# A macaron layer with attention and HGRN on one core: other orders in the SwiGLU and mix queues

## The reference

```python
x = x + 0.5 * swiglu_ffn(rms_norm(x, g1), w_gate1, w_up1, w_down1)    # D_FF = 2816
proj = rms_norm(x, gm) @ w_in                                          # 7 x 512 columns
aq, ak, av, hq, hf, hi, hg = split(proj)
A = chunked_band_attention(rms_norm(aq), rms_norm(ak), av, rel_bias)   # 8 heads x 64, 9-chunk key band
B = rms_norm(hgrn2(silu(hq), 1 - f, hi, log f)) * silu(hg)             # 4 heads x 128
x = x + concat(A, B) @ w_out
x = x + 0.5 * swiglu_ffn(rms_norm(x, g2), w_gate2, w_up2, w_down2)
```

## Time and profile before

| | us |
|---|---|
| runs of the kernel before | 1912.31, 1910.54, 1912.07 (median 1912.07) |
| the profiled execution | 1910.18 |
| its span in the trace | 1908.6 |
| busy in the span: PE / DVE / ACT / POOL | 1872.8 / 1130.3 / 675.0 / 419.2 |
| start, until the first product | 0 to 16.3 |
| FFN1: gate and up, then down | 16.3 to 457, then to 683 |
| mix | 683 to 1045 |
| attention | 1046 to 1167 |
| W_OUT, then FFN2 | 1168.7 to about 1270, then to the end |

### The profile page before, as it was taken

How to read it: one execution, slowest core, us unless ns; L and a number is a source line. 1 busy time by engine, 2 the same in 40 slices (tenths; PEclk the granted TensorE clock), 3 DMA queues, 4 the chain that set the end, 5 groups by cost and what they waited for, 6 DMA issues and landing times.

```text
span 1908.6 us, 24404 instructions
## 1 busy us (share of the span) xinstructions
PE 1872.8 (98%) x9160; PEld 1545.2 (81%) x9160; DVE 1130.3 (59%) x1583; ACT 675.0 (35%) x1027; POOL 419.2 (22%) x327
## 2 busy tenths in 40 slices
PE   9899999999999999999999999999999999999999
PEld 7688888888888888888887667887888888888887
DVE  6866666665556631157567774367666666655564
ACT  7332323233433534211223663263323232334332
POOL 2322342232103110002222310003224322421030
PEclk9999999999999999999999999999999999999999
DMA  5454545445866433433433510134545354468663
GB/s 169 149 175 151 169 140 177 149 149 210 338 195 196 130 122 117 137 115 132 137 121 99 175 59 1 47 108 149 177 149 177 133 183 143 155 224 315 221 192 138
DMA packets 221483, 297.04 MB, mean 156 GB/s; under 512 B 15392, under 2 KB 117928, under 8 KB 221376
## 3 DMA queue, kind: packets, MB, share of 16 engines
q1 hardware_dynamic: 206752, 262.19, 40.3%
q0 software_dynamic: 6272, 18.14, 2.9%
q10 hardware_dynamic: 8352, 15.27, 2.1%
HBM read 206.65 MB, written 92.56 MB: 157 GB/s over the span
## 4 chain that ended last, share of the span: by engine, by line
PE 91%; DVE 4%; issue 2%; ACT 1%; DMA 1%; POOL 0%; SPq 0%; DVEq 0%; ACTq 0%
PE ps L702 28%; PE ps L703 28%; PE ps L704 28%; PE ps L904 1%; PE ps L1001 1%; PE ps L736 1%; PE ps L988 1%; PE ps L1021 1%; DVE hK L1934 0%; PE ps L924 0%; DMA xs<-x 0%; PE ps L895 0%; DVE PT L2030 0%; DVE S L2019 0%; PE ps L927 0%
## 5 line engine op out<-in xcount | busy, mean ns | idle before, releaser
L702 PE MATMUL ps<-hThi,whi 128*128 128x512 f32 x896 | 350.8, 391 | 11.6 <-DVE hid L1685 9.8
L703 PE MATMUL ps<-hTlo,whi 128*128 128x512 f32 x896 | 349.4, 390 | 0.0
L704 PE MATMUL ps<-hThi,wlo 128*128 128x512 f32 x896 | 349.2, 390 | 0.0
L702 PE MATMUL ps<-whi 128*128 128x512 f32 x616 | 240.0, 390 | 0.0
L704 PE MATMUL ps<-whi,wlo 128*128 128x512 f32 x616 | 239.7, 389 | 0.0
L703 PE MATMUL ps<-wlo,whi 128*128 128x512 f32 x616 | 239.7, 389 | 0.0
L702 PEld LDWEIGHTS ps<-hThi,whi 128*128 128x128 f32 x896 | 168.6, 188 | 47.9 <-issue 12.6
L704 PEld LDWEIGHTS ps<-hThi,wlo 128*128 128x128 f32 x896 | 168.6, 188 | 35.1
L703 PEld LDWEIGHTS ps<-hTlo,whi 128*128 128x128 f32 x896 | 168.7, 188 | 34.4
L1652 DVE TENSOR_TENSOR wlo<-raw,whi 128x512 fp32r<-128x512 f32 x176 | 132.3, 755 | 97.5 <-ACT whi L1215 97.5
L702 PE MATMUL ps<-hXhi,whi 128*128 128x512 f32 x480 | 186.8, 389 | 0.0
(11 more groups left out here) (197 smaller groups left out, 2894.0 us busy)
## 6 DMA issues: line engine op xcount, KB each, us to landing
hid_scratch<-hid SPq DMA_DIRECT2D x132, 256.0 KB, 3.3
raw<-ffn_w_gate SPq DMA_DIRECT2D x44, 512.0 KB, 3.7
raw<-ffn_w_up SPq DMA_DIRECT2D x44, 512.0 KB, 4.9
wdb<-ffn_w_down SPq DMA_DIRECT2D x44, 512.0 KB, 3.9
wd_scratch<-wdb SPq DMA_DIRECT2D x88, 256.0 KB, 4.5
raw<-hid_scratch SPq DMA_DIRECT2D x80, 256.0 KB, 2.8
rawx<-hid_scratch SPq DMA_DIRECT2D x74, 256.0 KB, 2.8
raw<-w_in SPq DMA_DIRECT2D x28, 512.0 KB, 5.0
```

The lines of the kernel that those rows point to most:

```text
L702: pe.matmul(dst, ahi, bhi, start=first, stop=False, skip_group_check=onto)
L703: pe.matmul(dst, ahi, blo, start=False, stop=False, skip_group_check=onto)
L704: return pe.matmul(dst, alo, bhi, start=False, stop=last, skip_group_check=onto)
```

## The change

In words, part by part:

- Start: the gain comes as one row of 4 KB and is spread to 128 partitions by eight matmuls with a row of ones; ACT copies it from PSUM (`keep_gain`). 14 idle products in place of 24.
- The first product of each FFN, and the first tile of W_OUT, are issued in two passes (`late_tokens`): first all matmuls that need the tokens' hi part, then those with the lo part.
- SP, both FFNs: the weights of tile 3 go ahead of the first `load_down`; at e = 2 the stores of the hidden rows and their sums go ahead of `gate_up(4)`, `store_down_sums(0)` and `load_down(1)`.
- POOL, both FFNs: `hid_pair_sums(0)` goes ahead of `down_sums(0)`.
- DVE, both FFNs: the last `t34_lo` goes behind `plain_hid(0)`. At the end of FFN1 `hT_lo(R_MIX, 0)` goes ahead of `normalise(R_MIX, 3)`.
- Mix: the last tile is written out on its own (`last_tile`), with its features in the order 2 to 7, 0, 1. Both turns (q, k) come ahead of the readout; `scores(0)` is issued ahead of its last two features; ACT takes q and k ahead of tile 7's copy. DVE's sum of the readout (`read_sum`) and its use (`read_out`) move behind units 1 and 3.
- The four splits of w_out's first pieces on ACT and DVE move from that tile to units 37, 39, 41 and 43 of the last pair; `out_pieces(1)` on SP moves behind the loop over pairs.
- Attention's buffers are laid out in another order, banks of the first scores change from 6 to 4 for v = 1, and some semaphores are renamed or counted otherwise.

The diff, cut to its core:

```diff
@@ -580,20 +591,27 @@
                 for e in range(FT):
-                    if e + 2 < FT:
+                    if e == 0:
+                        gate_up(F, 2, w_gate, w_up)
+                        gate_up(F, 3, w_gate, w_up)
+                        load_down(F, 0, w_down)
+                    elif e + 2 < FT and e > NPLAIN:
                         gate_up(F, e + 2, w_gate, w_up)
-                    if e == 0:
-                        load_down(F, 0, w_down)
-                    elif e % 2:
+                    if e % 2:
                         store_hid(F, e - 1, A11)
-                        store_down_sums(F, e // 2)
-                        if e // 2 + 1 < NPAIR:
-                            load_down(F, e // 2 + 1, w_down)
-                    else:
+                        if e > NPLAIN:
+                            store_down_sums(F, e // 2)
+                            if e // 2 + 1 < NPAIR:
+                                load_down(F, e // 2 + 1, w_down)
+                    elif e:
                         store_hid(F, e - 1, A12)
...
                             store_hid_sum(F, e // 2 - 1, i)
+                    if e == NPLAIN:
+                        gate_up(F, e + 2, w_gate, w_up)
+                        store_down_sums(F, 0)
+                        load_down(F, 1, w_down)
                 for n in range(4):
...
@@ -702,6 +720,18 @@
+            def late_tokens(dst, stationary, moving, at, low_ready):
+                first = [(0, 0), (0, 1) if at == 0 else (1, 0)]
+                for k, (a, b) in enumerate(zip(stationary, moving)):
+                    for i, j in first:
+                        pe.matmul(dst, a[i], b[j], start=(k == 0 and (i, j) == (0, 0)), stop=False)
+                low_ready()
+                for k, (a, b) in enumerate(zip(stationary, moving)):
+                    mm = pe.matmul(dst, a[1 - at], b[at], start=False, stop=(k == len(moving) - 1))
+                return mm
...
@@ -757,10 +787,15 @@
                     if F:
-                        pe.wait_ge(hT_ready, TT * R + 4)
+                        pe.wait_ge(hT_hi_ready, TT * R + 4)
                         pe.wait_ge(z_copied, TT + 6)
                     else:
-                        pe.wait_ge(early_lo, 4)
+                        pe.wait_ge(early_hi, 4)
+                    late_tokens(bank(0), [[weight(a, w, F)[:, k * P:(k + 1) * P] for a in (whi, wlo)] for k in range(4)],
+                                [operand(0, k) for k in range(4)], 1,
+                                lambda: pe.wait_ge(hT_ready, TT * R + 4) if F else pe.wait_ge(early_lo, 4))\
+                        .then_inc(prod_done, 1)
+                    return
                 if (e, i) == (1, 0) and F:
...
@@ -829,7 +864,15 @@
             pe.wait_ge(mhalf_set, 2)
-            idle_products(24)
+            idle_products(4)
+            pe.wait_ge(gain1_ready, 16)
+            for h in range(2):
+                for c in range(4):
+                    at = h * HALF + c * P
+                    mm = pe.matmul(ps[:, 4 * HALF + at:4 * HALF + at + P], gn[0:1, :], gain_row[:, at:at + P],
+                                   start=True, stop=True)
+                mm.then_inc(gain1_spread, 1)
+            idle_products(10)
             pe.wait_ge(ident_loaded, 16)
...
@@ -853,10 +896,29 @@
-            def group(n0, advn, feature, hook):
+            def last_tile(n0, hook):
                 base = P_MIX + 4 * n0
-                for o in range(8):
+                pe.wait_ge(proj_evac, 8 * n0 + 4)
+                for at, k in enumerate(LAST_ORDER):
+                    s, c0 = slot(base + k // 2), (k % 2) * HALF
+                    a = [v[:, k, 7 * P:T] for v in (hThi, hTlo)]
+                    b = [w[:, s, c0:c0 + HALF] for w in (whi, wlo)]
+                    mm = three(bank(7), a, b, at == 0, at == KT - 1)
+                    if at in (2, 4, 6):
+                        mm.then_inc(piece_used, 1)
+                    if at in (3, 5, 7):
+                        mm.then_inc(proj_done, 1)
+                    if at == 3:
+                        hook(OUTER_AT)
+                    if at == 5:
+                        hook(READ_AT)
+                        scores(0)
+            def group(n0, advn, feature, hook, tiles=8):
+                base = P_MIX + 4 * n0
+                for o in range(tiles):
                     idx = 8 * n0 + o
...
@@ -956,14 +1018,13 @@
             def last_hook(at):
+                if at == READ_AT:
+                    pe.wait_ge(qkT_ready, 4)
                 last_head(at)
...
                     turn_qk(0, 0, 4)
-                if at == READ_AT:
-                    turn_qk(0, 1, 2)
-            group(3 + HH - 1, 0, False, last_hook)
+                    turn_qk(0, 1, 0)
...
@@ -1069,8 +1130,10 @@
+            group(3 + HH - 1, 0, False, last_hook, 7)
+            last_tile(3 + HH - 1, last_hook)
             for w in range(STEPS + 2):
-                if w < STEPS:
+                if 0 < w < STEPS:
                     scores(w)
...
@@ -1289,7 +1360,14 @@
-            for t in range(3):
+            def keep_gain(h):
+                act.wait_ge(gain1_spread, h + 1)
+                act.activation(gain[:, h * HALF:(h + 1) * HALF], bank(4 + h), ACT.Copy).then_inc(gain1_ready, 1)
+            keep_gain(0)
+            square(R_FFN1, 0)
+            keep_gain(1)
+            for t in range(1, 3):
                 square(R_FFN1, t)
...
@@ -1392,15 +1470,17 @@
                        .then_inc(k_rows, 1)
-                for q in range(4):
-                    used(n0, q, advn)
-                    split(P_MIX + 4 * n0 + 4 + q, 4 * advn)
-                    if q == 2 and square_at:
-                        act.wait_ge(proj_done, PROJ_OUTS)
-                        act.wait_ge(qk_gain_ready, 1)
-                        take_qk(0, 4)
-                evac(n0, advn, 7, func)
-                store(n0, advn, 7, feature)
+                if square_at:
+                    act.wait_ge(proj_done, QK_FREE)
+                    act.wait_ge(qk_gain_ready, 1)
+                    take_qk(0, 4)
+                    take_qk(1, 0)
+                else:
+                    for q in range(4):
+                        used(n0, q, advn)
+                        split(P_MIX + 4 * n0 + 4 + q, 4 * advn)
+                    evac(n0, advn, 7, func)
+                    store(n0, advn, 7, feature)
                 if head is not None:
...
@@ -1481,6 +1563,9 @@
                     keep_out(v // 2 - 2)
+                if v in OUT_SPLIT_AT:
+                    act.wait_ge(proj_done, MIX_DONE)
+                    split(P_OUT + OUT_SPLIT_AT.index(v))
                 if v < NV - NU and v % NU in SQUARE_AT:
...
@@ -1717,6 +1800,8 @@
                     plain_hid(F, e)
+                    if e == 0:
+                        t34_lo(F, 3)
                 if e >= NPLAIN and i == 5:
...
@@ -1812,15 +1897,17 @@
                 t34(0, j)
-            for j in range(4):
+            for j in range(3):
                 t34_lo(0, j)
...
                 down(0, n)
+                if n == 74:
+                    hT_lo(R_MIX, 0)
                 if 71 <= n < 75:
                     normalise(R_MIX, n - 71)
-                if n >= 75:
-                    hT_lo(R_MIX, n - 75)
+                if n == 75:
+                    hT_lo(R_MIX, 1)
             hT_lo(R_MIX, 2)
...
@@ -2022,6 +2110,8 @@
                 if v == 1:
+                    read_sum(HH - 1)
+                if v == 3:
                     read_out(HH - 1)
...
@@ -2136,7 +2228,9 @@
             def ffn(F):
-                for k in range(NPAIR):
+                hid_pair_sums(F, 0)
+                down_sums(F, 0)
+                for k in range(1, NPAIR):
                     down_sums(F, k)
...
```

More of the change, by code:

```diff
@@ L164 @@
 NV = NU * PAIRS
+OUT_SPLIT_AT = tuple(NV - NU + n for n in (1, 3, 5, 7))
 SQUARE_AT, SUM_AT, NORM_AT = (1, 4), (3, 5), (6, 8)
@@ L674, in _ @@
             load_v(1)
-            out_pieces(1)
             for p in range(2, PAIRS):
@@ L681, in _ @@
                 load_v(p)
+            out_pieces(1)
             for t in range(TT):
@@ L973, in scores @@
                     pe.wait_ge(unit_max, 2 * w)
-                else:
+                if w == 1:
                     pe.wait_ge(proj_evac, PROJ_OUTS)
@@ L1954, in head, with read_sum @@
                                                  ALU.mult, ALU.add).then_inc(state_step, 1)
-                for q in range(4):
-                    split(P_MIX + 16 + q, 4 * j)
+                if not prepare:
+                    for q in range(4):
+                        split(P_MIX + 16 + q, 4 * j)
+                    read_sum(j)
+                    read_out(j)
+            def read_sum(j):
                 dve.wait_ge(read_sq, j + 1)
```

63 lines of the change are left out of this document (36 added, 27 removed).

## The result

The changed kernel took 1919.87 us (median of four runs, 1919.69 to 1921.11) against 1912.19 for the kernel before beside it (1910.54 to 1912.72). The ratio of the runs is 1.0058, with a 95% interval of 1.0044 to 1.0072. Either way it is slower, by 7.7 us against the runs beside it and by some 10.8 against the later ones. The forecast was 1914.2, with "slower" at 0.32. The number lies at the very end of the stated range (1920.0) and outside the forecast's own (1910.5 to 1916.2): the likeliest case was wrong. The profiled executions are 1910.18 and 1920.05, with spans of 1908.6 and 1918.5, so the traces hold 9.9 us to be accounted for.

A forecast was written before the change was run, and what follows sets the result against it. TensorE (busy 1872.8 of 1908.6 us) bounds the kernel. Terms -4.6 + 2.6 - 1.07 - 1.06 - 0.45 + 6.7 = +2.1 turn 1910.18 into 1912.3, 1914.2 on the median's level; range 1905.5 to 1920.0, the forecast's own 1910.5 to 1916.2.

The forecast's parts named there:

- FFN2's longer stop: FFN2: five more DVE and POOL pairs fall ahead of L1685, so PE restarts later, +2.6 us (bounds -1.5 and +4).
- rival B: Slower: clock falls in FFN2 (+1.8) and once in the last pair (+2.2), giving 1918.2 us; chance 0.22.
- The splits: Attention's last pair: DVE's half waits for ACT's and delays the next maxima, four PE waits, +6.7 us (bounds +1, +8).
- FFN1's first stop: FFN1: earlier stores shorten PE's 7.62 us stop, DVE's queue becomes the limit; -4.6 us with the start (bounds -6.5, -3).
- The front: Front of attention: reordered turns, scores(0) and DVE steps bring scores(3) 0.45 us earlier, clock loss kept (bounds -2.7, +1).
- The start: Kernel start: gain row instead of broadcast, and first product no longer waiting for hTlo; -1.3 us together.
- gain 0.7: Start: x arrives with less traffic beside it, 0.7 us gained (bounds +1.3, and -0.6 if copies come late behind idle products).
- gain 0.6: First product: it waits for wlo, ready at 15.57, instead of hTlo, so 0.6 us is gained.
- I leave this loss in: FFN1: the 1.8 us clock loss behind the stop is kept, as the new stop is still about 5.2 us.
- I keep that loss too: Front of attention: the old front's 2.25 us clock loss is kept, as PE is as thinly used as before.
- A: Faster: the last pair's loop does not bind, splits cost 1 instead of 6.7, one clock loss goes; 1906.5 us, chance 0.22.
- C: Slower: FFN1's stop isn't shortened, POOL's contended sums hold the last store, PE restarts at 90; 1917.6 us, chance 0.10.

The follow-up runs named there:

- the later ones: 19 runs of the unchanged kernel before, shared by the first four follow-up experiments; median 1909.09 us.
- two experiments from opposite sides: Changed kernel with DVE's split halves two units behind ACT's: 1915.21 us; kernel before with only the splits and out_pieces(1) moved: 1917.38 us.
- a_d0_late: Changed kernel, but in both FFNs POOL's down_sums(0) waits for DVE's up1 of the third feature tile; 1904.85 us, ratio 0.9981 to the kernel before.
- a_ffn2_old: Changed kernel, with SP's, POOL's and DVE's order in FFN2 alone as in the kernel before; 1916.17 us, ratio 1.0038 to the kernel before.
- a_idle2: Changed kernel with 2 idle products instead of 10 behind the gain's spread matmuls; 1918.98 us, ratio 1.0059 to the kernel before.
- best_old_start: Changed kernel with down_sums(0) held for the third tile's up1, DVE's split halves two units later, and the old start; 1897.99 us, ratio 0.9940.
- a_d1_late: Changed kernel, but in both FFNs POOL's down_sums(1) waits for up1 of the fourth feature tile; 1921.45 us, ratio 1.0065 to the kernel before.
- b_stores_first: Kernel before, with only SP's stores of hid and its sums put ahead of tile 4's weights at e = 2; 1909.40 us, ratio 1.0002.
- b_split_moved: Kernel before, with only the four splits moved to units 37, 39, 41, 43 and out_pieces(1) behind the pairs loop; 1917.38 us, ratio 1.0037.

## Why the prediction was right or wrong

The steps that failed: the sum had no term for what the reorder of POOL and SP moves back, the second stops (+3.3 in both FFNs); it put the clock behind FFN2's longer stop at nothing, though rival B priced it (+2.9, and +0.6 in FFN1); and it priced the start at -1.3 where the trace shows +0.9, because the idle products were not counted ahead of the first turn (+2.2). The other terms held.

**The splits (+6.7):** right in mechanism, place and size (+6.4), shown by two experiments from opposite sides. In one detail it differs: the forecast has all four waits of PE for DVE's maxima; three of them are for PT, the copy that stands behind the delayed maximum in DVE's queue, and one is for a maximum. The forecast of each step (1.8, 1.3, 1.6, 2.0) and the waits (1.71, 1.04, 1.45, 1.78) agree in order too.

**FFN1's first stop (-4.6 with the start) and FFN2's (+2.6):** right in what sets them. The count of eight pairs at +1.1 gave the end of L1685 (now L1768) at 86.5 with a start 1.3 earlier than before; with the start 0.9 later that is 88.7, and it ended at 88.1. The trace shows the eight of POOL from 71.61 to 85.15. FFN2's restart was priced to 0.1. That POOL's wdb sums carry it is shown by a_d0_late, and that FFN2 only loses by a_ffn2_old.

**The front (-0.45, measured -0.6)** agrees in part by luck. The forecast keeps the clock as it was; in the changed kernel it stood at 0.50 for half as long (3.4 us for 6.8), and scores(2) took 2.08 instead of 2.51. What the order alone is worth there, no run took apart.

**The start (-1.3, measured +0.9)** failed at "gain 0.7": I priced x's arrival and the copies, and named idle products only as a cause of late copies. The first turn of x stands behind them in PE's queue. The first square did begin earlier (6.02 for 6.28) and DVE too (8.11 for 8.38), but PE was held by 20 idle matmuls until 11.4. They took 0.22 each; in the kernel before, the pace rose from 11 to 20 per 2 us at 6 us, and in the changed one not before 10. a_idle2 gives the 1.8 us back. The matmuls of one row that spread the gain are what differs ahead of the rise in pace. best_old_start, which takes them out, has the old pace again (20 in 6 to 8 us); in the three other profiles without them the pace also rises between 6 and 8, and in the eight with them not before 10. What in those matmuls does it stays open. Since the moment of the first product varies by up to 2.5 us under the changed kernel's start, the +0.9 is that of one execution. The term "gain 0.6" for late_tokens was right: in best_old_start the first product comes at 15.57 instead of 16.32.

**What the sum lacked:** the second stops (+1.9 and +1.4). The text said of SP's and POOL's order what comes earlier, and not what comes later: the wdb sums of pair 0 move back, their store behind them, then load_down(1), then down_sums(1), which lands on DVE's next sums of weights. a_d1_late shows that cause, though not its price.

**The clock** was rival B, with its place in FFN2 but not in the last pair: +2.9 in FFN2 where I had 1.8, +0.6 in FFN1, nothing in the last pair, whose grant stayed at 1.00 with PE standing still 1.0 to 1.8 us at a time. That was luck of the execution: in a_d0_late it fell there with the same waits. The step that failed is the sum itself, which holds no clock term for FFN2 ("I leave this loss in" and "I keep that loss too" stand for FFN1 and the front alone). I had priced FFN2's stop at 4.8 us, and FFN1's new one at 5.2, and let the same length cost 1.8 in one place and nothing in the other. The measured stops of 4.91 and 4.71 both brought 0.50; those of 2.65 (a_ffn2_old), 0.84 and 0.59 did not; those of 3.7 and 3.8 (b_stores_first) did. The Trainium skill (TensorE: Matmul & The Clock Gate, Part 1: The HAM clock gate) lets the outcome vary with the phase; this case bears it out in part. Whether the clock fell at an FFN's first stop shows no phase: over all twelve profiles the thirteen stops of 3.7 us and more brought 0.50, and the eleven of 2.65 and less did not. Elsewhere the outcome differs though the instructions there are the same: in the last pair, at the first products, and in the front of the changed kernel's order, where the spell is 3.4, 6.8 or 10.2 us long or, in a_d0_late, missing. That rule was in the text as a reason for a smaller sum; at the FFNs' stops the sum had to be larger.

**The rivals.** A was wrong: the loop bound in full. C was wrong: the stop did shrink, from 7.62 to 4.91. The misses add up: start +2.2, FFN1's stop -0.6, clocks +0.6 and +2.9, second stops +1.9 and +1.4, the five good terms -0.6 together, in all +7.8; with the forecast's +2.1 that is the trace's +9.9. B's 1918.2 was the nearest number in the text, but of its +4.0 the 2.2 of the last pair did not come, and the second stops and the start stood in for it.

## What to carry to other kernels

When an order is changed to bring one thing forward, price what goes back as well, and follow it one round on: here the sums that were moved back met a busy engine twice. Where two engines alternate over the same unit, extra work whose producer and consumer stand in the same step closes a loop; two units apart the same work cost 0.6 here instead of 6.4. An engine that fills idle time ahead of a deadline (idle matmuls) stands in a queue too, and its length must be priced at the slowest pace that the trace shows.

## What the runs showed of the hardware that I had not expected

The clock's cost behind a stop does not grow with the stop: 1.8 in the kernel before for 7.6 us, 2.4 in the changed one for 4.9. A stretch of the kernel before, then three of the changed one, in FFN1 (columns as in rows 9):

```profile
94.00:96.00 2.00, 2.00 (x8) 1.59 (x7) 1.14 (x2) 0.00 (x0) 1.92 (x2) 0.79 0.00 0
```
```profile
86.00:88.00 2.00, 0.00 (x0) 0.00 (x0) 2.00 (x4) 0.00 (x0) 0.00 (x0) 0.59 1.03 399
88.00:90.00 2.00, 1.75 (x4) 1.49 (x5) 2.00 (x5) 0.00 (x0) 0.00 (x0) 0.50 0.33 125
92.00:94.00 2.00, 2.00 (x7) 1.57 (x7) 0.45 (x1) 0.00 (x0) 0.00 (x0) 0.71 0.61 250
```

A grant of 0.59 in 86 to 88 and 0.71 in 92 to 94 puts the spell at 0.50 from about 86.4 to 93.2, with PE back at 88.25. Before, it ran from about 88.0 (1.00 in 86 to 88, 0.50 in 88 to 90) to 94.8, with PE back at 91.28. Both spells last 6.8 us; what one costs is the part behind the restart. Here the shorter stop left more of it to pay. The length is not fixed: in b_split_moved the spell behind the same stop lasted 10.2 us, and in b_stores_first the one behind FFN2's stop 3.4.

The pace of the small matmuls at the start doubled at 6 us in the kernel before and only after 10 in the changed one, while the granted clock reads 1.00 through both. The kernel before, then the changed one:

```profile
4.00:6.00 2.00, 2.00 (x11) 2.00 (x11) 0.00 (x0) 0.00 (x0) 0.00 (x0) 1.00 1.02 326
6.00:8.00 2.00, 2.00 (x20) 2.00 (x19) 0.00 (x0) 1.16 (x3) 0.40 (x2) 1.00 1.02 391
```
```profile
8.00:10.00 2.00, 2.00 (x11) 2.00 (x11) 0.94 (x2) 1.91 (x4) 0.82 (x3) 1.00 1.12 341
10.00:12.00 2.00, 2.00 (x15) 2.00 (x14) 1.28 (x2) 0.11 (x2) 0.97 (x2) 1.00 1.14 343
```

So that column does not tell the pace in the first microseconds; the count behind PE's busy time does. With the old start back and the spread matmuls gone (best_old_start):

```profile
6.00:8.00 2.00, 2.00 (x20) 2.00 (x19) 0.00 (x0) 1.22 (x3) 0.45 (x2) 1.00 1.02 392
```
